# Gate products between attention steps: halves of twelve matmuls behind every second step in place of quarters of six behind each

## The reference, cut to what matters

```python
y_a = sliding-window attention with sinks and bias    # 8 heads, 2 key/value groups
y_b = latent attention (MLA), 8 heads, latent width 128, rotary key of 32
g = sigmoid(x @ w_gate + b_gate)                      # (640, 1024) @ (1024, 2048)
h = g[..., :1024] * (y_a @ w_proj_a) + g[..., 1024:] * (y_b @ w_proj_b)
x = layer_norm(ALPHA * x + h @ w_out)
x = layer_norm(ALPHA * x + conv_glu(x))
```

## Time and profile before

| | us |
|---|---|
| median of 3 runs | 2094.05 (2093.67 to 2097.93) |
| the profiled execution, its own time | 2092.84 |
| its span, first to last instruction | 2090.9 |
| granted TensorE clock, mean of the span | 0.959 |
| TensorE busy | 1918.7 (92%) |
| attention stages (from the first L1406 to the last attention matmul) | 172.4 to 425, and 1183.2 to 1439 |

### The profile page before, as it was taken

How to read it: one execution, slowest core, us unless ns; L and a number is a source line. 1 busy time by engine, 2 the same in 40 slices (tenths; PEclk the granted TensorE clock), 3 DMA queues, 4 the chain that set the end, 5 groups by cost and what they waited for, 6 DMA issues and landing times.

```text
span 2090.9 us, 33733 instructions
## 1 busy us (share of the span) xinstructions
PE 1918.7 (92%) x12626; PEld 1803.5 (86%) x12626; DVE 977.6 (47%) x1429; ACT 665.1 (32%) x1319; POOL 675.5 (32%) x312
## 2 busy tenths in 40 slices
PE   6787999989899999999899789998997999999992
PEld 6685778889799999999898667887997999999992
DVE  3346534445754432443354563344466543234336
ACT  2123333342244311332232242334323442122222
POOL 2231111114633334333722211111372433343275
PEclk9899999999999999999999999999999999999996
DMA  4323122232112112211231412222320211222121
GB/s 126 135 73 129 43 94 84 75 122 106 61 61 81 65 61 96 81 57 59 71 131 40 139 40 83 100 74 104 111 81 33 92 72 61 86 81 80 50 81 65
DMA packets 56416, 171.67 MB, mean 82 GB/s; under 512 B 8024, under 2 KB 22024, under 8 KB 48072
## 3 DMA queue, kind: packets, MB, share of 16 engines
q1 hardware_dynamic: 56296, 170.07, 23.5%
HBM read 151.52 MB, written 18.28 MB: 81 GB/s over the span
## 4 chain that ended last, share of the span: by engine, by line
PE 70%; issue 14%; POOL 6%; DVE 5%; ACT 2%; DMA 2%; SPq 0%; POOLq 0%; DVEq 0%; ACTq 0%
PE ps L1297 49%; PE ps L1519 11%; POOL w_lo L582 5%; PE ps L1422 2%; PE ps L1445 2%; DMA gates<-gate_logits 1%; PE ps L1492 1%; PE ps L1431 1%; POOL sum_sq L606 1%; ACT probs L707 1%; PE ps L1429 1%; PE ps L1496 1%; PE ps L1378 1%; DVE probs L1055 1%; ACT logits L740 1%
## 5 line engine op out<-in xcount | busy, mean ns | idle before, releaser
L582 POOL TENSOR_TENSOR w_lo<-w_raw,w_hi 128x1024 fp32r<-128x1024 f32 (+3 forms) x252 | 577.3, 2300 | 1394.4 <-ACT w_hi L664 1383.4
L664 ACT ACTIVATE w_hi<-w_raw 128x1024 fp32r<-128x1024 f32 (+3 forms) x248 | 234.9, 968 | 455.3 <-PE ps L1297 432.1
L1297 PE MATMUL ps<-x_hi,w_hi 128*128 128x320 f32 x1504 | 345.6, 311 | 29.8 <-POOL w_lo L582 29.8
L1297 PE MATMUL ps<-x_lo,w_hi 128*128 128x320 f32 x1504 | 344.7, 311 | 0.0
L1297 PE MATMUL ps<-x_hi,w_lo 128*128 128x320 f32 x1504 | 344.2, 310 | 0.0
L1297 PEld LDWEIGHTS ps<-x_hi,w_hi 128*128 128x128 f32 x1504 | 253.0, 189 | 31.5 <-ACT w_hi L664 24.0
L1297 PEld LDWEIGHTS ps<-x_lo,w_hi 128*128 128x128 f32 x1504 | 253.5, 189 | 0.0
L1297 PEld LDWEIGHTS ps<-x_hi,w_lo 128*128 128x128 f32 x1504 | 253.3, 189 | 0.0
L1519 PE MATMUL ps<-x_hi,w_hi 128*128 128x320 f32 x512 | 190.8, 373 | 19.0 <-ACT logits L740 18.8
L1201 DVE TENSOR_SCALAR f_conv<-f_ext,vec 128x656 f32<-128x656 f32 x44 | 67.2, 1528 | 225.2 <-ACT tail L840 223.3
L1519 PE MATMUL ps<-x_hi,w_lo 128*128 128x320 f32 x512 | 162.1, 317 | 0.0
(11 more groups left out here) (221 smaller groups left out, 3043.5 us busy)
## 6 DMA issues: line engine op xcount, KB each, us to landing
w_raw<-in_slabs SPq DMA_DIRECT2D x88, 1024.0 KB, 4.9
w_raw<-in_slabs SPq DMA_DIRECT2D x20, 768.0 KB, 4.2
gate_logits<-logits SPq DMA_DIRECT2D x64, 160.0 KB, 1.8
gates<-gate_logits SPq DMA_DIRECT2D x16, 640.0 KB, 7.2
w_raw<-in_slabs SPq DMA_DIRECT2D x16, 640.0 KB, 3.9
ckvc<-in_ckvc SPq DMA_DIRECT2D x16, 256.0 KB, 2.7
ckvc_t<-in_ckvc_t SPq DMA_DIRECT2D x16, 256.0 KB, 2.9
x_in<-in_x_t SPq DMA_DIRECT2D x4, 640.0 KB, 8.7
```

The costliest lines, as they stand in the source:

```text
L582: pool.tensor_tensor(w_lo[:, s % 2, c], w_raw[:, s % 2, c], w_hi[:, s % 2, c].bitcast(F32), ALU.subtract).then_inc(wlo_ready, 1)
L664: A(w_hi[:, s % 2, c], w_raw[:, s % 2, c], ACT.Copy).then_inc(whi_ready, 1)
L1297: ins = MM(out_[:, a, :], w, x[:, t, a * HT:(a + 1) * HT], start=t == 0 and w is wh and x is hi, stop=t == tiles - 1 and w is wl)
```

## The change

- A group is now 2 halves of 12 matmuls. Four halves stand ahead of `turn(0)`, as eight quarters did. After that a half stands behind every second step: the places are numbered n = 3 * u + step, and only an even n has one (`halves_behind`). For an even u these are (u, 0) and (u, 2), for an odd u it is (u, 1).
- `gate_ends(g)` follows: 4 * g - 6 in place of 4 * g - 5. A group ends one place earlier, with two attention steps between its end and the start of the next group, where there was one.
- `quarter_at_scores` follows. It moves the loads of the caches of r = 2, 4 and 6 from quarters 63, 81 and 99 of SP's list to 64, 82 and 100, so that of r = 2 comes behind the slab load and the store at quarter 63.
- The number, shapes and order of the gate matmuls are the same, and so are all steps of the attention. `UNITS` isn't in the diff: mixer B's prompt is divided as before.

```diff
-assert 4 * NG == 8 + 3 * NU
+assert 2 * NG == 4 + 3 * NU // 2
+
+
+def halves_behind(u, step):
+
+    n = 3 * u + step
+    return [] if n % 2 else [4 + n // 2]
 
 
 def gate_ends(g):
 
-    return divmod(4 * g + 3 - 8, 3)
+    return divmod(4 * g - 6, 3)
 
 
 def quarter_at_scores(u):
-    return 0 if u < 2 else 8 + 3 * (u - 2) + 1
+    return 0 if u < 2 else 2 * (4 + (3 * (u - 2) + 2) // 2)
...
-                def gate_quarter(c):
-
-                    g, q = divmod(c, 4)
+                def gate_half(h):
+
+                    g, q = divmod(h, 2)
...
-                    for t in (2 * q, 2 * q + 1):
+                    for t in range(4 * q, 4 * q + 4):
...
-                    if q == 3:
+                    if q == 1:
                         ins.then_inc(gate_done, 1)
 
                 scores(0)
                 scores(1)
-                for c in range(8):
-                    gate_quarter(c)
+                for h in range(4):
+                    gate_half(h)
                 for u in range(NU):
                     turn(u)
-                    gate_quarter(8 + 3 * u)
+                    for h in halves_behind(u, 0):
+                        gate_half(h)
                     if u + 2 < NU:
                         scores(u + 2)
-                    gate_quarter(9 + 3 * u)
+                    for h in halves_behind(u, 1):
+                        gate_half(h)
                     values(u)
-                    gate_quarter(10 + 3 * u)
+                    for h in halves_behind(u, 2):
+                        gate_half(h)
```

## The result

The changed kernel takes 2060.2 us (median, 2058.9 to 2064.1) against 2093.9 before; the ratio is 0.984, 95% interval 0.982 to 0.986. The direction and the places were right, the size was half of what came.

What follows compares the result with a forecast made beforehand. TensorE, busy 92% of the span, was taken as the bound, with DVE and ACT bounding the Ap units. Per layer 3.5 + 3.1 + 1.0 - 0.3 + 1.0 = 8.3 us, 16.6 in two, gave 2077.5 us; range 2065 to 2091.

Steps and rivals of the forecast that it cites:

- Part 1: Ap units: earlier takes shorten waits, turn(5) 4.8 us earlier; 3.5 us a layer gained, bounds 1 and 5.
- One sign that was named for being wrong: First attention stage: low clock from 192 to 228 us would show the forecast wrong.
- Part 2: Units after Ap: all short waits for ACT's take go, 3.1 us a layer gained, bounds 1.5 and 3.1.
- The feared starvation of odd units: Later units: uneven spacing, some 3.5 us after an odd As unit's turn against 5.4, might make vector work late; slack over 1.5.
- Part 3: Joins of attention steps without a gate block between: bubbles mostly stay, 1 us a layer gained.
- free joins: Attention steps running together without bubbles: 8 us a layer gained, less in fact.
- Part 4: SP's list: scores(17) stall 2.6 instead of 2.32 us, low clock stays, 0.3 lost a layer; stream 2's cache costs nothing.
- Part 5: End of the stage: one quarter's tail leaves the path to the projections, 1.0 us a layer gained, bounds 0.5 and 1.5.
- A: Rival: joined attention steps run without bubbles, up to 7 us a layer more, 2063 us; chance 0.10.
- B: Rival: removed Ap waits reappear at turns or values with low clock; 3.5 us a layer, 2087, at worst 2091; chance 0.22.
- C: Rival: low clock holds in the Ap units up to unit 8, 4.2 us a layer slower, 2102; chance 0.04.
- D: Rival: stream 2's cache comes late, scores(23) stall and the clock falls, gain gone, 2094; chance 0.04.

Runs made afterwards that it cites:

- the clean comparison: Stream 0's cache load sent ahead of the slab load, in the kernel before (2079.4 us) and the changed kernel (2052.1 us), compared from turn(8) to the projections.
- 30 fewer blocks: Blocks of 6, 6 and 12 with stream 0's cache load ahead of the slab load, 2054.5 us, against halves with the same load edit, 2052.1 us.
- the version without the cache wait: Stream 0's three cache DMAs sent ahead of load_gate(6): 2079.4 us from the kernel before, 2052.1 us from the changed kernel.

## Why the prediction was right and wrong

**Part 1, Ap units: the mechanism held.** Turn(5) came 5.0 us earlier against turn(0), for 4.8 by hand. The hand count's stall at values(4) was 0.73 and not 1.7, the one at (5, 1) 1.71 for 1.5. To unit 8 it was 4.2 and 4.4 us, 4.5 by hand. The 3.5 put into the sum was a deduction for low clock behind the new waits. In the first layer none came behind them, in the second 3.4 us behind the wait at (5, 1). One sign that was named for being wrong did come: low clock between 192 and 228 us, but 3.4 us of it and behind the wait at group 3, which is in both kernels (194 to 198 in the first layer of the changed kernel, columns as in the earlier trace rows):

```profile
194.00:198.00 4.00, 4.00 (x20) 2.92 (x19) 3.40 (x7) 0.89 (x3) 0.00 (x0) 0.57 0.12 43
```

Over these units the low clock is 6.8 and 10.2 us in the two layers before and 3.4 and 6.8 after. Missed: 1.6 us over both layers.

**Part 2, takes of later units: the term was mis-sized, 3.1 for 5.5.** I summed the bracketed idle times. But a matmul's end is modelled, some 0.15 to 0.3 us behind the point at which the next one could start, so the bracket leaves out that part, and a wait shorter than it isn't shown. The kernel before, PE timeline, a turn with a take's wait behind it and one without:

```profile
237.18 0.38 PE L1445 MATMUL ps<-ident,probs 128*128 128x128 f32 x2
238.15 0.38 PE L1519 MATMUL ps<-x_hi,w_hi 128*128 128x320 f32 x1 [0.58 <-ACT logits L740]
...
242.71 0.38 PE L1445 MATMUL ps<-ident,probs 128*128 128x128 f32 x2
242.85 0.39 PE L1519 MATMUL ps<-x_hi,w_hi 128*128 128x320 f32 x1
```

From the turn to its quarter it is 0.97 us with the wait and 0.14 without: 0.83 us lost, for 0.58 in the bracket. Adding up such differences for the 24 groups that start behind a step from unit 8 on gives 5.7 us in the first layer: 5.0 at the nine waits with a bracket, which show 3.1, and 0.7 at four without one. All but 0.2 of it goes. What stays is at (13, 1), where a turn and the scores of an As unit stand between end and start: the half there starts 0.38 us behind the scores' last record, elsewhere 0.18. So "the take has 1 us or more in every place" was wrong there. The feared starvation of odd units didn't come: no wait for probabilities shows behind unit 8.

**Part 3, joins: 1.0 taken, 2.0 measured.** 8.5 us of the clean comparison less 5.5 for takes and 1.0 for the end leaves 2.0 a layer for 60 fewer blocks, far from the 8 of free joins; the 1.0 for 30 fewer blocks measured above fits it. Chain of the changed kernel in two As rounds, in order: half, turn, scores (L1421, L1422), half, values (L1489, L1490), turn, half:

```profile
237.67 1.95 PE ps L1524 x12
239.62 0.22 PE ps L1450 x2
239.84 0.37 PE ps L1421 x4
240.21 0.07 PE ps L1422 x4
240.28 1.98 PE ps L1524 x12
242.26 0.26 PE ps L1489 x2
...
243.29 0.37 PE ps L1450 x2
243.65 1.75 PE ps L1524 x12
```

A half behind scores or values costs 1.95 to 1.98, one behind a turn 1.75, as its parts did. A turn behind values costs 0.37 instead of 0.22: the bubble moves from the gate block to the turn (by 0.15, more than the 0.1 that the prediction allowed for). Scores behind a turn cost nothing more, 0.37 as behind a quarter. The same steps in the chain of the kernel before:

```profile
247.83 0.22 PE ps L1445 x2
...
248.93 0.37 PE ps L1416 x4
```

So the bubbles stay with the change of shape for the most part, as argued. The rule of the Trainium skill, "TensorEngine Tiling (Array Packing)", "Key Properties", that a change of tiling mode drains the TensorE, agrees: joined steps of different shapes pay as before.

**Part 4, SP's list: the wait right, its consequence wrong.** The stall came as 2.2 to 2.3 us (2.6 forecast) and stream 2's cache wasn't waited for. The sentence that failed is "the low clock behind it stays". From turn(8) to the projections the excess over the version without the cache wait was 6.7 us a layer before, and 2.5 and 5.7 after. So 4.2 and 1.0 us were gained where I had put a loss of 0.3. I had read the length of the low spell from one trace as a constant. In the changed kernel it was 0 to 7 us in four cases where before it was 10 in four. It varies with the execution; that the short take wait inside it, which the change took away, is the reason for the 10 isn't shown, and what sets the length stays open.

**Part 5, the end: right.** From the end of TensorE's last work of the stage (424.00 + 1.09) to the projections it was 7.15 us, and it is 6.15 now, from the end of values(39) at 410.18. The other 1.1 us of the table's last row are the quarter that now stands ahead of turn(39).

Summed up over both layers, the missing 14.8 us of the span are: takes 4.8, cache wait and its clock 5.8, Ap 1.6, joins 2.0, outside the stages 2.1, less 1.5 for low clock at the start of the first stage. What lies outside the stages and the low clock at the start are chance as far as the traces tell, and so is a part of the cache wait's 5.8, since the spell varies with the execution. Of the rivals, A's figure of 2063 was near the result for a wrong reason, since joins were not free; B, C and D didn't come. The range was too narrow because two terms that I took from a single reading, the bracketed waits and the low spell, had no bound upwards for the gain.

## What to carry to other kernels

When one PSUM bank is shared by a filler product, end its groups two steps ahead of the next start and split them only as finely as the copies need cover: halves were better than blocks of 6, 6 and 12 by 1 us a layer, whole groups worse by 20 us in all. Price a short wait on TensorE from start to start against the same pair of steps without it, not by the idle time shown, and put the low clock that may follow into the bounds in both directions. A small load that is wanted soon should not stand behind a slab load that waits for someone: moving three DMAs in a queue was worth 8 us in the changed kernel and 14 in the kernel before.

## What the runs showed of the hardware

- A wait of 1.8 to 2.5 us with a busy TensorE around it was followed by the 1.2 GHz level in 19 of 20 cases at the cache wait, for 3 to 10 us; the twentieth had none. Each microsecond at that level cost about 0.47 us in the halves order (turn(15) to turn(17): 12.73 with none, 14.33 with 3 and 15.92 with 7 us).
- The same program had different low spells in two executions (0 and 7, 7 and 3 us). By the 0.47 above that is worth 1.4 us (an estimate); the changed kernel's times spread over 7 us, 2057 to 2064, and what makes the rest isn't shown.
- The level at the start of a stage also varies: 9.87 us from the first scores to turn(0) without low clock, 11.40 with it, in the same kernel's two layers. What decides it stays open.
